# First and last FFN groups with stationary tokens, two residual column groups turned on VectorE and ScalarE, output scaled in quarters

## What is computed

```python
x = x + hybrid_mixer(rms_norm(x, norm1_g), ...)          # ends with  [ret, lru] @ w_out
x = x + cross_attend(rms_norm(x, norm2_g), memn, ...)    # begins with xn @ wq, ends with o @ wo
x = x + conv_ffn(rms_norm(x, norm3_g), w_up, conv_w, conv_b, w_down)
return rms_norm(x, final_g)

def conv_ffn(xn, w_up, conv_w, conv_b, w_down):
    h = causal_dwconv(xn @ w_up, conv_w, conv_b)          # 3 taps along the tokens
    a, b = jnp.split(h, 2, axis=-1)
    return (jax.nn.silu(a) * b) @ w_down
```

## Time and profile before

| | |
|---|---|
| median of 3 runs | 1497.08 us (1497.0 to 1497.7) |
| the profiled execution, its own time | 1496.23 us |
| its span, first to last instruction | 1494.4 us |
| PE busy | 1484.4 us (99%) |
| DVE busy / ACT busy | 1030.6 us (69%) / 920.0 us (62%) |
| mean granted TensorE clock | 0.998 of 2.4 GHz |
| HBM read | 286.19 MB, mean 193 GB/s |

### The profile page before, as it was taken

The page is one execution under the profiler, slowest core; times in us unless marked ns, Lnnn a source line. Parts: engine busy times, 40 slices in busy tenths (PEclk is TensorE's granted clock), DMA queues, the critical chain, the costliest instruction groups (busy, mean ns, idle before and its releaser), DMA issues.

```text
span 1494.4 us, 22743 instructions
## 1 busy us (share of the span) xinstructions
PE 1484.4 (99%) x7350; PEld 1256.4 (84%) x7350; DVE 1030.6 (69%) x1415; ACT 920.0 (62%) x1383; POOL 2.9 (0%) x9
## 2 busy tenths in 40 slices
PE   9999999999999999999999999999999999999997
PEld 8888888888888888888888888888888888888886
DVE  6756666788887556665567576675867667586886
ACT  6644578744555546554565668586766858676654
POOL 0000000000000000000000000000000000000000
PEclk9999999999999999999999999999999999999999
DMA  9766655665557565446546565556556565656564
GB/s 349 254 201 211 208 188 186 202 196 170 169 168 250 172 190 160 157 144 195 192 160 208 184 200 186 194 187 203 184 197 196 192 191 189 197 185 197 182 197 141
DMA packets 80459, 288.90 MB, mean 193 GB/s; under 512 B 8944, under 2 KB 10480, under 8 KB 79520
## 3 DMA queue, kind: packets, MB, share of 16 engines
q1 hardware_dynamic: 76176, 275.68, 57.1%
q10 hardware_dynamic: 3744, 9.30, 1.8%
q0 software_dynamic: 496, 3.34, 0.6%
HBM read 286.19 MB, written 2.10 MB: 193 GB/s over the span
## 4 chain that ended last, share of the span: by engine, by line
PE 96%; DVE 2%; ACT 1%; issue 1%; DMA 0%; ACTq 0%; DVEq 0%
PE ps L280 95%; DVE wlo L981 1%; ACT whi L584 0%; PE ps L341 0%; DVE vm L1506 0%; DMA hl<-in_first_in 0%; DVE xres L1516 0%; ACT xT L608 0%; ACT scr L791 0%; PE ps L442 0%; DVE tmp L999 0%; ACT scr L824 0%; ACT scr L958 0%; DVE sm_ L1333 0%; DVE xres L1482 0%
## 5 line engine op out<-in xcount | busy, mean ns | idle before, releaser
L981 DVE TENSOR_TENSOR wlo<-raw,whi 128x1024 fp32r<-128x1024 f32 x516 | 624.2, 1221 | 297.2 <-ACT whi L584 288.5
L584 ACT ACTIVATE whi<-raw 128x1024 fp32r<-128x1024 f32 x516 | 530.8, 1052 | 241.4 <-PE ps L280 233.9
L280 PE MATMUL ps<-whi,mixT 128*128 128x512 f32 x1472 | 457.4, 390 | 0.4 <-ACT whi L625 0.4
L280 PE MATMUL ps<-xT,whi 128*128 128x512 f32 x1152 | 399.2, 398 | 0.8 <-DVE wlo L981 0.5
L280 PE MATMUL ps<-whi,xT 128*128 128x512 f32 x1280 | 396.1, 389 | 0.0
L280 PEld LDWEIGHTS ps<-whi,mixT 128*128 128x128 f32 x1472 | 276.2, 188 | 57.8 <-issue 0.5
L280 PE MATMUL ps<-xT,wlo 128*128 128x256 f32 x1152 | 303.6, 278 | 0.0
L280 PE MATMUL ps<-wlo,mixT 128*128 128x512 f32 x736 | 285.1, 389 | 0.0
L280 PEld LDWEIGHTS ps<-whi,xT 128*128 128x128 f32 x1280 | 240.2, 188 | 50.0
L280 PE MATMUL ps<-wlo,xT 128*128 128x512 f32 x640 | 249.0, 389 | 0.0
L280 PEld LDWEIGHTS ps<-xT,whi 128*128 128x128 f32 x1152 | 210.0, 188 | 43.4 <-DVE wlo L981 2.0
(11 more groups left out here) (186 smaller groups left out, 748.4 us busy)
## 6 DMA issues: line engine op xcount, KB each, us to landing
raw<-in_stream SPq DMA_DIRECT2D x518, 512.0 KB, 3.4
xres<-in_xin ACTq DMA_DIRECT2D x2, 1024.0 KB, 7.0
scr<-in_xt_in ACTq DMA_DIRECT2D x8, 256.0 KB, 3.6
xres<-in_xin POOLq DMA_DIRECT2D x1, 2048.0 KB, 12.0
out_x<-vm SPq DMA_DIRECT2D x4, 512.0 KB, 3.1
raw<-in_stream SPq DMA_DIRECT2D x4, 256.0 KB, 4.2
kT<-in_memt_in ACTq DMA_DIRECT2D x2, 512.0 KB, 5.3
vbuf<-in_memin ACTq DMA_DIRECT2D x1, 1024.0 KB, 9.7
```

The costliest lines, as they stand in the source:

```text
L280: return nc.tensor.matmul(o, l, r, start=start, stop=stop, skip_group_check=True)
L584: A(whi[:, 2 * pr + s, :], raw[:, 2 * pr + s, :], ACT.Copy).then_inc(hi_done, 1)
L981: V.tensor_tensor(wlo[:, 2 * pr + s, :], raw[:, 2 * pr + s, :], f32(whi[:, 2 * pr + s, :]), ALU.subtract).then_inc(lo_done, 1)
```

## The change

- **FFN groups 0 and 10** are computed like groups 1 to 9, wide. Group 0's chunks take in the wait for the last normed tiles and the transposes of column group 7. The order of the weight stream becomes gate and up of groups 0 and 1, then down of group g-1 behind gate and up of g up to g = 8, then groups 9 and 10 one after the other, then down of 8, 9 and 10. Two groups then follow another without a down product between, so the second half of their tap work runs in the first steps of the group behind (`tail == "full"`). `row_of(2)`, `diag_of` and all the code of `pair` are gone; the scale of the rows is `rcol` itself.
- **Column groups 0, 1, 4 and 5** of the normed residual are turned by DVE (`turn_stage`, 2 block transposes of 128x512) and ACT (`move_stage`, 16 copies of 32x256), spread over the steps of the second half of the projection; PE keeps the transposes of groups 2, 3, 6 and 7.
- **The residual sum is written in place**, in `xres`; the buffer `stage` and the copies `keep` go.
- **The end**: the third quarter of each row gets gain and scale in one DVE instruction after the rms is known; DVE scales the first quarter, ACT the fourth and the second, and there are eight stores of 256 KB.

```diff
+        def stage(g, tt):
+            return xres[:, tt, (g % 4) * CG:(g % 4 + 1) * CG]
...
             for tt in range(TT):
-                for n in range(2):
-                    sp.wait_ge(out_ready[n], tt + 1)
-                    sp.dma_start(out[tt * P:(tt + 1) * P, n * R:(n + 1) * R],
-                                 zout[:, tt, n * R:(n + 1) * R]).then_inc(out_sem, 16)
+                for i, n in enumerate((0, 3, 2, 1)):
+                    sp.wait_ge(out_ready[i % 2], 2 * tt + (i // 2 + 1))
+                    sp.dma_start(out[tt * P:(tt + 1) * P, n * CG:(n + 1) * CG],
+                                 zout[:, tt, n * CG:(n + 1) * CG]).then_inc(out_sem, 16)
...
-                    mid = (lambda g=2 * half - 1 + n // 7: norm_tr(g)) if n == 7 or (n == 0 and half) else None
+                    mid = (lambda: norm_tr(2)) if n == 7 and half else None
...
-            narrow(C_F // 2, 0, xT, NEXT, 8)
-            narrow(C_F // 2, 1, xT, {6: lambda: [row_of(2), 4][1]})
-            up(C_F // 2 + 1, 2 * GF - 2)
-            with pe.Fori(1, NG - 1) as g:
+            up_wide(C_F // 2, 0, True)
+            up_wide(C_F // 2, 1)
+            with pe.Fori(1, NG - 2) as g:
                 m = C_F // 2 - 2 + 6 * g
                 up_wide(m, 0)
                 up_wide(m, 1)
                 down(m + 4, g)
-
-            up(NC // 2 - 8, 2 * GF, 2)
-            down(NC // 2 - 4, NG - 1)
-            down(NC // 2 - 2, NG, GF, 2)
+            for m in (NC // 2 - 14, NC // 2 - 10):
+                up_wide(m, 0)
+                up_wide(m, 1)
+            down(NC // 2 - 6, NG - 2)
+            down(NC // 2 - 4, NG - 1, GF)
+            down(NC // 2 - 2, NG, 2 * GF, 2)
...
+            def move_stage(g, *parts):
+
+                i = 2 * (g // 4) + g % 2
+                act.wait_ge(stage_turned, 2 * i + 2)
+                for i in parts:
+                    for q in range(4):
+                        A(st_turned[g % 2][q * 32:(q + 1) * 32].rearrange("p j (t i b) -> p j t i b", t=TT, i=4)[:, :, :, i, :],
+                          st_blocks[i * 32:(i + 1) * 32, q], ACT.Copy).then_inc(stage_moved, 1)
...
+                step(m + 4, 0, None, lambda: move_stage(g0, 0), lambda: move_stage(g0, 1))
+                step(m + 4, 1, None, lambda: move_stage(g0, 2), lambda: move_stage(g0, 3))
+                step(m + 5, 0, None, lambda: [turned_hi(g0, gain, b) for b in range(2)], lambda: move_stage(g1, 0))
+                step(m + 5, 1, None, lambda: move_stage(g1, 1), lambda: move_stage(g1, 2))
+                step(m + 6, 0, None, lambda: move_stage(g1, 3), lambda: turned_hi(g1, gain, 0))
+                step(m + 6, 1, None, lambda: turned_hi(g1, gain, 1))
+                step(m + 7, 0, None, lambda: norm_hi(g0 + 2, gain), lambda: stage_squares(g0 + 2))
...
             def ffn_pass(m, g, tail=None, downs=True, k0=0):
...
+                if full:
+                    at(0, None, lambda: move_blocks(g - 1, 1, 0), lambda: move_blocks(g - 1, 1, 1))
+                    at(1, None, lambda: move_blocks(g - 1, 1, 2), lambda: move_blocks(g - 1, 1, 3))
+                    at(2, lambda: set_taps(g - 1, 1, 0), lambda: set_taps(g - 1, 1, 2), lambda: silu4(g - 1))
...
                 at(3, lambda: keep_rows(0))
                 at(4, None, lambda: move_blocks(g, 0, 0), lambda: move_blocks(g, 0, 1))
-                at(5, None, lambda: move_blocks(g, 0, 2), lambda: move_blocks(g, 0, 3))
+                at(5, (lambda: hidden_hi(g - 1, k0)) if full else None,
+                   lambda: move_blocks(g, 0, 2), lambda: move_blocks(g, 0, 3))
...
             def add_stage(g):
-                if g >= 2:
-                    dve.wait_ge(stage_kept, 4 * (g - 1))
                 for tt in range(TT):
-                    V.tensor_tensor(stage[:, g % 2, tt, :], ps[:, 2 * (g % 2) + tt, :],
-                                    xres[:, tt, (g % 4) * CG:(g % 4 + 1) * CG], ALU.add).then_inc(stage_ready, 1)
+                    V.tensor_tensor(stage(g, tt), ps[:, 2 * (g % 2) + tt, :], stage(g, tt), ALU.add).then_inc(stage_ready, 1)
...
+                step(m + 3, 0, lambda: add_stage(g0), None, lambda: turn_stage(g0))
+                step(m + 3, 1, lambda: add_stage(g1))
+                step(m + 4, 0)
+                step(m + 4, 1)
+                step(m + 5, 0, None, lambda: turn_stage(g1), lambda: [turned_lo(g0, gain, b) for b in range(2)])
...
-                V.tensor_scalar(zout[:, tt, :R], zout[:, tt, :R], rcol[:, 4, tt:tt + 1], None,
+                third = slice(2 * CG, 3 * CG)
+                V.tensor_scalar(zout[:, tt, :CG], zout[:, tt, :CG], rcol[:, 4, tt:tt + 1], None,
                                 ALU.mult).then_inc(out_ready[0], 1)
+                V.scalar_tensor_tensor(out=zout[:, tt, third], in0=xres[:, tt, third], scalar=rcol[:, 4, tt:tt + 1],
+                                       in1=gfin[:, third], op0=ALU.mult, op1=ALU.mult).then_inc(out_ready[0], 1)
```

More of the change, by code:

```diff
@@ L336, in norm_tr @@
                 for j in range(4):
-                    if j % 2 == 0 and not isinstance(g, int) or g > 0:
+                    if j % 2 == 0:
                         pe.wait_ge(nt_lo, 4 * g - 2 + j // 2 * 2)
@@ L789, in stage_squares @@
                     if g + tt:
-                        act.wait_ge(stage_kept, 4 * g + tt)
-                    A(junk[:], stage[:, g % 2, tt, :], ACT.Square,
-                      accum_out=ssum[:, tt, g % 4:g % 4 + 1]).then_inc(stage_kept, 1)
-            def keep(g):
-                for tt in range(TT):
-                    A(xres[:, tt, (g % 4) * CG:(g % 4 + 1) * CG], stage[:, g % 2, tt, :], ACT.Copy).then_inc(stage_kept, 1)
+                        act.wait_ge(stage_squared, 2 * g + tt)
@@ L799, in norm_hi @@
+                    A(junk[:], stage(g, tt), ACT.Square, accum_out=ssum[:, tt, g % 4:g % 4 + 1]).then_inc(stage_squared, 1)
             def norm_hi(g, gain):
                 for b in range(2):
-                    act.wait_ge(nt_tr, 2 * g + b + 1)
+                    act.wait_ge(nt_tr, 4 * (g // 4) + 2 * (g % 2) + b + 1)
                     hi_tiles(two((bankA, bankB)[b]), xT, gain, (4 * g + 2 * b) % KT, nt_hi)
             junk = scr[:, 6:8, :].rearrange("p a b -> p (a b)")
-            def wide_norm(c0, g0, gain, extra, extra2={}):
-                for half in range(2):
-                    for n in range(8):
-                        m, pr, g = c0 // 2 + 4 * half + n // 2, n % 2, g0 + 2 * half + n - 6
-                        if n >= 6:
-                            if half and n == 7:
-                                step(m, pr, None, lambda: norm_hi(g, gain), lambda: (stage_squares(g), sqrt_ms(2 + g0 // 4)))
-                            else:
-                                step(m, pr, None, lambda: norm_hi(g, gain), lambda: (stage_squares(g), keep(g)))
-                        else:
-                            step(m, pr, None, extra.get((half, n)), extra2.get((half, n)))
@@ L862, in keys @@
                     keys_hi(h)
-                step(m, 0, lambda: take(0), None, values if tail else lambda: keep(3))
+                step(m, 0, lambda: take(0), None, values if tail else None)
                 step(m, 1, lambda: take(1), keys)
@@ L938, in ffn_pass @@
-                at(9, None, lambda: move_blocks(g, 1, 2), lambda: move_blocks(g, 1, 3))
-                at(10, lambda: set_taps(g, 1, 0), lambda: set_taps(g, 1, 2), lambda: silu4(g))
-                at(11)
-            act.wait_ge(fpar_in, 16)
-            for k in range(GF):
-                pair(C_F // 2 + k, 0, k, 0, None if k else lambda: keep(7))
-            ffn_pass(C_F // 2 + 4, 1, False)
-            with act.Fori(2, NG - 1) as g:
-                ffn_pass(C_F // 2 - 2 + 6 * g, g, True)
@@ L948, in _ @@
-            for k in range(GF):
-                pair(NC // 2 - 8 + k, NG - 1, k, GF, None if k else lambda: hidden4_hi(NG - 2))
+                if downs:
+                    at(8, None, lambda: move_blocks(g, 1, 0), lambda: move_blocks(g, 1, 1))
+                    at(9, None, lambda: move_blocks(g, 1, 2), lambda: move_blocks(g, 1, 3))
+                    at(10, lambda: set_taps(g, 1, 0), lambda: set_taps(g, 1, 2), lambda: silu4(g))
+                    at(11)
+            act.wait_ge(fpar_in, 16)
@@ L950, in _ @@
+            act.wait_ge(tok_scale, 1)
+            ffn_pass(C_F // 2, 0, None, False)
+            ffn_pass(C_F // 2 + 4, 1, "full")
+            with act.Fori(2, NG - 2) as g:
+                ffn_pass(C_F // 2 - 2 + 6 * g, g, "short")
+            ffn_pass(NC // 2 - 14, NG - 2, "short", False)
+            ffn_pass(NC // 2 - 10, NG - 1, "full", True, GF)
             for n in range(NCG):
-                step(NC // 2 - 4 + n // 2, n % 2)
+                step(NC // 2 - 4 + n // 2, n % 2, None, None, None if n else lambda: hidden_hi(NG - 1, 2 * GF))
@@ L970, in _ @@
                 act.wait_ge(fin_rms, tt + 1)
[L971 removed]
+                for n in (3, 1):
```

(2 more changed lines are left out.)

238 lines of the change are left out of this document (107 added, 131 removed).

## The result

| | before | after |
|---|---|---|
| median | 1497.08 us (5 runs, 1496.57 to 1497.74) | 1489.04 us (5 runs, 1488.80 to 1489.79) |
| profiled execution, its span | 1496.23, 1494.4 us | 1489.79, 1488.0 us |
| mean granted TensorE clock | 0.998 | 0.999 |

The ratio of the times is 0.9946, with an interval of 0.9932 to 0.9961: 8.0 us less, where 8.5 were forecast. The kernel is faster, and the time lies 0.4 us above the forecast of 1488.6.

What follows compares the result with a forecast made beforehand. PE was taken as the bound, busy 1484.4 us of a 1494.4 us span. Gains of 3.6 + 1.8 + 2.4 + 0.7 = 8.5 us from the 1497.08 us median gave 1488.6 us, range 1486.6 to 1492.2.

Steps and rivals of the forecast that it cites:

- Part 1: Residual transposes: four of eight lots leave PE at 0.90 us each, gaining 3.6 us (bounds 2.8 to 4.2).
- Parts 2 and 3: FFN groups 0 and 10 computed wide instead of narrow: 1.8 us and 2.4 us gained.
- rival two: FFN groups 0 and 10: the narrow pace stays after widening, total gain 6.7 us, 1490.4 us; chance 0.06.
- Part 4: Kernel's end: earlier rms and smaller first piece let the first of the last stores start sooner, gaining 0.7 us.
- Part 5: Work moved onto ACT and DVE, in projections and FFN groups 1 and 10: costs nothing if PE never waits.
- pinch (one): FFN groups 1 and 10: ACT-DVE hand-overs use up 0.7 us slack, PE waits; most likely 1491.5 us; chance 0.10.
- wait for group 7's tiles (four): Before the first FFN chunk PE waits for column group 7's tiles: about 1493.6 to 1495 us; chance 0.03.
- rival three: Both projections: longer moves make ACT the bound and PE waits; 1505.8 us at d = 0.35; chance 0.03.
- its formula: Both projections: a move longer by d costs 2 x (32 d + 0.5 - 3.1) us; the 8.5 gain is gone at d = 0.21.
- the slack of 3.1 us: Projection steps: ACT's delay before PE waits for a weight panel, counted to when PE ends the chunk or half chunk.

Runs made afterwards that it cites:

- pe_turns_all: The changed kernel, but PE transposes all eight column groups again, with the residual sum still in place: 1492.76 us, ratio 0.9975.
- moves_plus1: The changed kernel with one extra 32x256 copy in every lot of four ACT moves in both projections: 1492.11 us, ratio 0.9967.
- moves_plus2: The changed kernel with two extra 32x256 copies in every lot of four ACT moves in both projections: 1499.31 us, ratio 1.0014.

## Why the prediction was right

**Part 1, right.** 3.6 us forecast, 3.6 by `pe_turns_all`; in the trace each lot is worth 0.92 us (1.83 / 2) in the first piece.

**Parts 2 and 3, right in sum.** 4.2 forecast, 4.3 measured without part 1. The new chunks run at 5.44 us with PE never idle, so rival two is refuted. But what I said against it, that both shapes keep their own pace in every steady stretch, was wrong: before's group 10 ran at 5.65 us (chunk ends at 1431.74, 1437.39 and 1443.06), which stood in the same trace. Eight chunks at 5.55 would have given 8 x 0.11 = 0.9 us and eight at 5.65 give 8 x 0.21 = 1.7; with the 0.5 us in which PE was idle that is most of the 2.4. The number was right since it came from the marks of the whole stretch and not from pace times count.

**Part 4, mis-sized.** 0.7 us forecast, with bounds of -0.7 and +1.9. The trace shows 0.24 lost, the medians show nothing (0.06 between the two ends). The failing step is "what counts is about when the first starts". The first store did start 0.6 us sooner, nearly the 0.7 that I had worked out; but I took the rate as given. Quarters flow at about 320 GB/s, halves at about 390, and a store of 256 KB lands 3.1 us after its issue, no sooner than one of 512 KB. The rows hinted at it: the earlier trace rows has 3.1 us for 512 KB and 4.2 us for loads of 256 KB, and I took the middle. The Trainium skill, "DMA: Bandwidth & Descriptors", section "Bandwidth", advises transfers of 1 MiB or more, for smaller ones reach less of the peak (its figures are for loads, issued by GpSimd). The stores here agree in direction, with 320 GB/s at 256 KB and 390 at 512 KB.

**Part 5, right.** The forecast had ACT late by 0.24, 0.5, 0.9, 1.1 and 0.5 in the projections; it was 0.12, 0.37, 0.33, 0.57 and 0. The tiles from SBUF took 0.42 us each in place of up to 0.50, and the copies overlap by a little. In group 10 it was 1.4 for 1.5. An ACT table load of 1.28 us in group 1 (at 826.14) was not in the reckoning; cover hid it. No rival came true: no pinch (one), no wait for group 7's tiles (four), and ACT short of its limit (three). The moves in the projections take 415 ns, as in the FFN, so rival three had nothing to start from. But its formula was somewhat too kind: an added copy is d = 0.415 / 4 = 0.10 us a move and gives 2 x (3.3 + 0.5 - 3.1) = 1.4 us where `moves_plus1` cost 3.0; two give 8.1 where `moves_plus2` cost 10.2. The term that is too large is the slack of 3.1 us: PE loads a panel's weights 0.46 us before I had it due, and copies that stand between a step's two splits delay the second panel by 0.415 us each. With 3.1 - 0.46 - 0.42 = 2.2 and, for two copies, 1.8, the formula gives 2 x (3.3 + 0.5 - 2.2) = 3.2 and 2 x (6.6 + 0.5 - 1.8) = 10.6. This was worked out afterwards from the two runs, and no third run tests it.

**The sum.** 3.6 + 1.8 + 2.4 + 0.7 = 8.5 forecast; 1.83 + 6.08 - 0.24 = 7.7 in the trace, 8.0 in the medians. The miss in part 4 is 0.9 us and the runs of one kernel scatter by about 1 us, so the total could not show it; the marks did. No version here beats the change by more than the runs scatter: 1489.02 with ACT's last store, 1489.14 with the change itself, 1489.20 with the old end.

## What to carry to other kernels

Where one engine bounds a kernel, find starts that mark its progress in another engine's timeline and price the change by whole stretches between them; for the stretches that PE bounds that held to 0.1 us here, where pace times count would have missed 1.5 us in one group. Work laid under such an engine is free up to a limit that can be worked out from the rows, if the slack is counted to the weight load and not to the first matmul, and past it the cost comes at once: 0 with four copies a lot, 3 us with five, 10 with six. At a kernel's end a store that starts sooner because it is smaller may land no sooner.
